# A two-layer decoder trunk on one NeuronCore: straight-line layers, weight rings in half-unit pieces, another opening and seam

## The reference, cut to what matters

```python
h = rms_norm(x, norm_g)
proj = h @ w_in                          # 1024 -> many columns
q_lat, kv_lat, z_a, dn_qkv, dn_a, dn_b, z_b, dil_qkv, z_c, gate_logits = split(proj)
y_a = mla_branch(q_lat, kv_lat, ...)     # latent attention, 4 heads; two more small projections (q_b, kv_b)
y_b = gated_deltanet_branch(dn_qkv, dn_a, dn_b, ...)   # convolution, chunked delta rule
y_c = dilated_branch(dil_qkv, ...)       # three groups of windowed attention
ys = stack([y_a * silu(z_a), y_b * silu(z_b), y_c * silu(z_c)])
branch_out = einsum('bsnc,ncd->bsnd', ys, w_branch)
mixed = sum(sigmoid(gate_logits) * branch_out)
x = x + mixed @ w_out
```

## Time and profile before

| | us |
|---|---|
| three timed runs | 909.52, 910.36, 913.64 |
| median | 910.36 |
| span of the profiled execution | 909.1 |
| TensorE busy | 863.2 (95%) |
| VectorE busy | 601.9 (66%) |
| ScalarE busy | 499.4 (55%) |
| GpSimd busy | 266.5 (29%) |
| chain that ended last: TensorE / issue / GpSimd / VectorE | 70% / 14% / 6% / 5% |

### The profile page before, as it was taken

How to read it: one execution, slowest core, us unless ns; L and a number is a source line. 1 busy time by engine, 2 the same in 40 slices (tenths; PEclk the granted TensorE clock), 3 DMA queues, 4 the chain that set the end, 5 groups by cost and what they waited for, 6 DMA issues and landing times.

```text
span 909.1 us, 13835 instructions
## 1 busy us (share of the span) xinstructions
PE 863.2 (95%) x4578; PEld 730.4 (80%) x4578; DVE 601.9 (66%) x766; ACT 499.4 (55%) x1034; POOL 266.5 (29%) x240
## 2 busy tenths in 40 slices
PE   4988999899999999999989799998899999999997
PEld 4977788778888887788778677887788888877886
DVE  5477669786566466486645874798675745765773
ACT  5776456437566554345357764655573855443542
POOL 1234012693516001241112520237543330114120
PEclk9999999999999999999989999999999999999999
DMA  8544334442524344345274243444334242443551
GB/s 252 161 135 175 106 127 139 139 135 69 167 94 133 101 138 152 127 156 215 64 215 155 93 160 119 139 140 133 105 134 134 84 154 93 139 152 127 185 185 47
DMA packets 67821, 124.51 MB, mean 137 GB/s; under 512 B 5165, under 2 KB 12327, under 8 KB 67623
## 3 DMA queue, kind: packets, MB, share of 16 engines
q1 hardware_dynamic: 67191, 122.30, 41.5%
q10 hardware_dynamic: 560, 1.30, 0.4%
HBM read 122.55 MB, written 1.05 MB: 136 GB/s over the span
## 4 chain that ended last, share of the span: by engine, by line
PE 70%; issue 14%; POOL 6%; DVE 5%; ACT 2%; DMA 1%; SPq 0%; POOLq 0%; DVEq 0%; ACTq 0%
PE bank L624 17%; PE bank L626 17%; PE bank L625 17%; POOL sm L1523 3%; PE bank L756 2%; PE bank L818 2%; PE bank L826 2%; PE bank L728 2%; PE bank L710 2%; DVE w_lo L1148 2%; PE bank L825 1%; PE bank L737 1%; PE bank L726 1%; PE bank L725 1%; PE bank L654 1%
## 5 line engine op out<-in xcount | busy, mean ns | idle before, releaser
L1148 DVE TENSOR_TENSOR w_lo<-raw,w_hi 128x1024 fp32r<-128x1024 f32 (+4 forms) x240 | 315.4, 1356 | 111.9 <-ACT w_hi L903 108.9
L624 PE MATMUL bank<-w_hi,hT 128*128 128x512 f32 (+2 forms) x800 | 318.3, 398 | 17.2 <-DVE w_lo L1148 7.2
L626 PE MATMUL bank<-w_hi,hT 128*128 128x512 f32 (+2 forms) x800 | 310.6, 388 | 0.0
L625 PE MATMUL bank<-w_lo,hT 128*128 128x512 f32 (+2 forms) x800 | 310.3, 388 | 0.0
L903 ACT ACTIVATE w_hi<-raw 128x1024 fp32r<-128x1024 f32 (+4 forms) x240 | 230.7, 1015 | 79.5 <-PE bank L626 78.1
L624 PEld LDWEIGHTS bank<-w_hi,hT 128*128 128x128 f32 x800 | 152.4, 191 | 50.2 <-DVE w_lo L1148 14.6
L626 PEld LDWEIGHTS bank<-w_hi,hT 128*128 128x128 f32 x800 | 152.0, 190 | 29.7
L625 PEld LDWEIGHTS bank<-w_lo,hT 128*128 128x128 f32 x800 | 152.4, 190 | 26.2
L1523 POOL TENSOR_TENSOR sm<-sm,tab 128x8 f32<-128x8 f32 (+2 forms) x72 | 64.5, 897 | 267.6 <-ACT at L982 110.3
L1107 ACT ACTIVATE at<-at,sm 128x128 f32<-128x128 f32 (+1 forms) x64 | 32.8, 514 | 69.1 <-DVE sm L1374 50.0
L624 PE MATMUL bank<-w_hi,yT 128*128 128x512 f32 (+1 forms) x136 | 54.8, 403 | 2.0 <-DVE w_lo L1148 2.0
(11 more groups left out here) (201 smaller groups left out, 1101.3 us busy)
## 6 DMA issues: line engine op xcount, KB each, us to landing
raw<-in_w_in SPq DMA_DIRECT2D x84, 1024.0 KB, 5.0
raw<-in_w_branch SPq DMA_DIRECT2D x12, 1024.0 KB, 5.1
raw<-in_w_out SPq DMA_DIRECT2D x8, 1024.0 KB, 5.0
raw<-in_w_in SPq DMA_DIRECT2D x4, 768.0 KB, 6.8
raw<-in_w_in SPq DMA_DIRECT2D x4, 640.0 KB, 8.2
raw<-in_mla_w_q_b SPq DMA_DIRECT2D x4, 576.0 KB, 3.9
raw<-in_mla_w_kv_b SPq DMA_DIRECT2D x4, 512.0 KB, 3.8
tab<-in_tables ACTq DMA_DIRECT2D x1, 1152.0 KB, 7.8
```

What stands on the lines that cost most here:

```text
L624: mm(o, src[0][:, k0 + k, tok], hi[:, k, :], start=starts and k == 0, stop=False)
L625: mm(o, src[0][:, k0 + k, tok], lo[:, k, :], start=False, stop=False)
L626: last = mm(o, src[1][:, k0 + k, tok], hi[:, k, :], start=False, stop=ends and k == nk - 1)
L1148: tt(view(w_lo, u % SPLIT, nk, n)[:, a:b, :], view(raw, u % RAW, nk, n)[:, a:b, :], view(w_hi, u % SPLIT, nk, n)[:, a:b, :].bitcast(F32), ...
```

## The change

It does the following.

- Both layers are written out: `ORDER` is a list of (layer, step), the loops are gone and all semaphore values are constants.
- The unit of both rings is a piece, half a unit (2 of 4 chunks; 2 and 1 of 3 for qb; 1 and 1 of 2 for kvb). The raw ring has 4 pieces (before 6), the split ring 5 (before 4). A `unit` step is now one piece; after piece q comes the `prep` of piece q + 4, which waits until TensorE is done with piece q - 1. Within a piece all chunks of t = 0 run first, then those of t = 1; so a block's bank 0 is complete half a piece before the block's end.
- latkv comes before latq. dn_g0, dn_g1, lat_norm move to unit 3 and dn_gc to unit 4.
- The opening: SP issues x first; the parameter loads go to ScalarE's queue, as does the second table load right behind; the rows' copy and the factor 0.5 are made by ScalarE; sine and exponential table come after the first four pieces' splits; VectorE's angle steps are merged; five small warm-up matmuls.
- The seam: xT 0 and 1 of the next layer come after the first unit of out1; xT 2, 3, norm and m_tables come between the two pieces of the next layer's unit 0. Layer 1's gain loads stand on SP behind the pieces of units 0 and 1 and wait for out1's adds.
- mT 2 and 3 come between the pieces of unit 56. GpSimd adds mixed per token tile. The output is stored in four parts.

```diff
-RAW, SPLIT = 3, 2
+RAW, SPLIT = 4, 5
+WARM = (3, 2)
-    us = halves("latq", 0, Q_RANK + 2 * H) + halves("latkv", 0, KV_RANK + ROPE) + halves("dn", 0, W)
+    us = halves("latkv", 0, KV_RANK + ROPE) + halves("latq", 0, Q_RANK + 2 * H) + halves("dn", 0, W)
-    put(1, ("dn_g0",), ("dn_g1",))
-    put(2, ("dn_gc",))
-    put(3, ("lat_norm",))
+    put(3, ("dn_g0",), ("dn_g1",), ("lat_norm",))
+    put(4, ("dn_gc",))
+def build_order():
+    steps, middle = step_table(), middle_table()      # middle_table: {56: [("mT", 2), ("mT", 3)]}
+    order = [(0, ("xT", 0)), (0, ("xT", 1)), (0, ("prep", 0, 0)), (0, ("prep", 0, 1)), (0, ("xT", 2)), (0, ("xT", 3)),
+             (0, ("prep", 1, 0)), (0, ("prep", 1, 1)), (0, ("norm",)), (0, ("m_tables",))]
+    def ahead(layer, u, p):
+        q = piece_at(layer, u, p) + SPLIT - 1
+        return [(q // (PIECES * NU), ("prep", q // PIECES % NU, q % PIECES))] if q < PIECES_ALL else []
+    for layer in range(DEPTH):
+        for u in range(NU):
+            order.append((layer, ("unit", u, 0)))
+            order += ahead(layer, u, 0)
+            if u == 0 and layer > 0:
+                order += [(layer, ("xT", 2)), (layer, ("xT", 3)), (layer, ("norm",)), (layer, ("m_tables",))]
+            order += [(layer, s) for s in middle.get(u, [])]
+            order.append((layer, ("unit", u, 1)))
+            order += ahead(layer, u, 1)
+            if whole(u) or UNITS[u][2] == 1:
+                order.append((layer, evict_step(u)))
+            order += [(layer, s) for s in steps[u]]
+            if u == NU - 2 and layer + 1 < DEPTH:
+                order += [(layer + 1, ("xT", 0)), (layer + 1, ("xT", 1))]
+    return order
...
 # SyncE
+                    for p in range(PIECES):
+                        q = piece_at(layer, u, p)
+                        if q >= RAW:
+                            sp.wait_ge(lo_done, q - RAW + 1)
+                        ...
-                    if u == RAW - 1:
-                        sp.wait_ge(*layer_start(layer))
+                    if u == 1:
+                        if layer > 0:
+                            sp.wait_ge(*out_taken(1, layer - 1))
                         for name, src in (("mq", mla_q_norm_g), ...
 # TensorE, one piece
+                pe.wait_ge(lo_done, q + 1)
                 for t in range(NT):
                     if starts:
                         pe.wait_ge(*free(step, layer, t))
...
+                    for k in range(k1 - k0):
+                        a = at_k + k0 + k
+                        mm(o, src[0][:, a, tok], hi[:, k, :], start=starts and k == 0, stop=False)
+                        mm(o, src[0][:, a, tok], lo[:, k, :], start=False, stop=False)
+                        last = mm(o, src[1][:, a, tok], hi[:, k, :], start=False, stop=last_piece and k == k1 - k0 - 1)
...
 # ScalarE, prep
+                act.wait_ge(raw_loaded[q % RAW], 16 * RAW_AT[q])
+                if q >= SPLIT:
+                    act.wait_ge(*used(q - SPLIT))
 # TensorE, transposes of x
-                if step[1] == 0:
-                    pe.wait_ge(*layer_start(layer))
-                pe.wait_ge(start[f"x_loaded{step[1] // 2}"], 16)
+                if layer > 0:
+                    pe.wait_ge(*out_taken(step[1] // 2, layer - 1))
+                else:
+                    pe.wait_ge(start[f"x_loaded{step[1] // 2}"], 16)
...
```

More of the change, by code:

```diff
@@ L195, in banks @@
     if k == "unit":
-        what, _, hf, _, _ = UNITS[a[0]]
-        return [0, 1] if hf == 0 else []
+        return [0, 1] if UNITS[a[0]][2] == 0 and a[1] == 0 else []
     if k in ("xT", "mT"):
@@ L494, in after, with used, block_taken, out_taken @@
         def after(engine, step, layer):
-            return part(engine, step), layer * COUNT[step[0]] + PLACE[step] + 1
+            return part(engine, step), PLACE[(layer, step)] + 1
         def bank_unit(u):
[L500 to L516, removed]
+            return ("unit", u - UNITS[u][2], 0)
+        def used(q):
+            layer, u, p = q // (PIECES * NU), q // PIECES % NU, q % PIECES
+            if ends(u, p):
+                return full(bank_unit(u), layer, 1)
+            return piece_done, q + 1 - layer * ENDS - sum(ends(v, PIECES - 1) for v in range(u))
+        def block_taken(u, layer, t=1):
+            return taken(bank_unit(u), layer, t)
+        def out_taken(i, layer):
+            return block_taken(unit_of("out", i), layer)
         def unit_of(what, i):
@@ L600, in unit @@
             def unit(step, layer):
-                u = step[1]
+                _, u, p = step
                 what, i, hf, nk, n = UNITS[u]
-                hi, lo = view(w_hi, u % SPLIT, nk, n), view(w_lo, u % SPLIT, nk, n)
-                starts, ends = whole(u) or hf == 0, whole(u) or hf == 1
-                src, k0 = (yT, 3 if what == "kvb" else 0) if whole(u) else (hT, hf * nk)
+                q = piece_at(layer, u, p)
+                k0, k1 = piece(nk, p)
+                hi, lo = view(w_hi, q % SPLIT, k1 - k0, n), view(w_lo, q % SPLIT, k1 - k0, n)
+                starts, last_piece = (whole(u) or hf == 0) and p == 0, ends(u, p)
+                src, at_k = (yT, 3 if what == "kvb" else 0) if whole(u) else (hT, hf * nk)
                 if what == "qb":
@@ L612, in unit @@
                 pair = "xT" if u < 2 else "mT" if what == "out" and i == 0 else None
+                if pair:
+                    pe.wait_ge(*taken((pair, (at_k + k0) // 2), layer))
+                pe.wait_ge(lo_done, q + 1)
                 for t in range(NT):
@@ L1506, in _ @@
             last.then_inc(start["rot_ready"], 1)
-            dve.wait_ge(start["rows_copied"], 1)
-            with dve.Fori(0, DEPTH) as layer:
-                for step in ORDER:
-                    if step[0] in parts:
-                        parts[step[0]](step, layer)
+            for layer, step in ORDER[ORDER.index((0, ("norm",))):]:
+                if step[0] in parts:
+                    parts[step[0]](step, layer)
         @block.gpsimd
@@ L1538, in evict @@
                 what, i, hf, nk, n = UNITS[u]
-                pool.wait_ge(*block_taken(u, layer))
-                m = mixed[:, :, (i % 2) * n:(i % 2 + 1) * n]
-                tt(m, m, gate, ALU.add).then_inc(part("gpsimd", step), 1)
+                for t in range(NT):
+                    pool.wait_ge(*taken(bank_unit(u), layer, t))
+                    m = mixed[:, t, (i % 2) * n:(i % 2 + 1) * n]
+                    last = tt(m, m, gate[:, t, :], ALU.add)
+                last.then_inc(part("gpsimd", step), 1)
             def norm(step, layer):
```

295 lines of the change are left out of this document (141 added, 154 removed).

## The result

The changed kernel takes 921.91 us (median of 4 runs, 921.2 to 924.89) where the kernel before takes 910.84 (4 runs beside it, 909.52 to 913.64): a ratio of 1.012, 95% interval 1.009 to 1.0151. It is slower by about 11 us, outside the 0.5% that a measurement tells. The profiled execution's span is 919.0 us (before 909.1), so 9.9 us are to be found in the trace. (A timed execution of the changed kernel lies 2.2 us above its own span, one of the kernel before 1.8 us; the rest of the 11 is scatter.)

The account below looks back on a forecast made before the run. TensorE, busy 863.2 of 909.1 us, was taken to bound the kernel, leaving some 46 us of idle time and slow matmuls to win. Terms summed to +9.3 on the median of 910.4, given as 919.5; range 902 to 927.

Parts of the forecast that it names:

- Opening: Start until dn0: loads, then ScalarE's splits and norm let q_lat begin at about 24.0 us; +0.9 us.
- qb and kvb: qb and kvb blocks, both layers: ScalarE's split ahead, waiting for its slot, delays the evictions; +4.8 us.
- The ring's gain: DeltaNet stretch, both layers: the deeper ring removes a w_lo wait, GpSimd then limits; -1.2 us.
- Late evictions: Five blocks a layer at branch and output: VectorE's split work delays evictions, 0.57 us each; +5.7 us.
- mT: First output half, both layers: moving the transposes of mixed inside it removes a 1.18 us wait; -2.4 us.
- Seam: Between layers: gain loads delay layer 1's fifth piece, whose split holds ScalarE ahead of xT 2 and 3; +1.9 us.
- "not held" bound: Between layers: the lower bound if ScalarE were not held by the fifth piece's split; -6.6 us.
- Straight-line code: Whole kernel: writing out the loop in itself changes nothing, bounds 0 and +5 us.
- the first (loads and splits ahead as meant): Faster rival: layer 1's fifth piece lands before xT 2, the seam gains 6.6 us; 897 us, chance 0.18.
- The second, losses hidden: Rival: qb-stage and VectorE eviction losses are hidden, nothing to measure; 912 us, chance 0.20.
- Slow starts: Rival: each stop of the qb and kvb stage adds 2.6 us of slow matmuls, four places; 930 us, chance 0.07.
- Loads bounding the ring: Rival: 240 piece loads of 512 KB, one behind the other, set the time; about 926 us, chance 0.05.

Follow-up runs that it names:

- run 7: The changed kernel with the positions' load second on ScalarE's queue, ahead of the parameter loads; 921.91 us, ratio 1.0121.
- Run 8: The changed kernel with four instead of five pieces in the split ring, each split one piece later in the order; 922.28 us, ratio 1.0134.
- run 10: The changed kernel with the split three pieces ahead instead of four, the split ring still of five; 916.2 us, ratio 1.0051.
- run 5: The changed kernel with the eviction ahead of the second piece's split only from unit 47 on (branch5 to out1); 917.9 us, ratio 1.0097.
- run 12: The changed kernel with splits three pieces ahead, layer 1's gain loads behind unit 3, and the tails' evictions ahead of the second split; 909.44 us, ratio 0.9993.
- Run 1: The changed kernel with layer 1's seven gain loads behind the pieces of unit 3 instead of unit 1; 914.95 us, ratio 1.0025.
- Run 4: The kernel before with its five loops over the layers written out and nothing else; 905.71 us, ratio 0.9937.
- run 11: The changed kernel with the split three pieces ahead and layer 1's gain loads behind unit 3; 909.43 us, ratio 0.9975.
- run 6: The changed kernel with the eviction ahead of the second piece's split for the two qb units alone; 928.86 us, ratio 1.0217.

## Why the prediction was right

The forecast of 919.5 was 2.4 below the measured 921.9, and inside its range; the ratio's interval (+8 to +14 us) holds it. (The terms add up to +9.3, and 910.4 + 9.3 is 919.7, not 919.5.) The mechanisms of the three largest losses, at the seam, in the qb stage and at the late evictions, are in the trace as described; that the sum comes so close is partly luck, since errors cancel. So term by term:

- **Opening, +0.9 against +0.6.** The amount held, the working did not. I had it bound by loads until 14.0; but the loads of the first stretch were in, and what was late was VectorE, whose chain of angles could begin only at 8.89, when the positions had landed as the sixth load of ScalarE's queue. It ran to 13.26 ahead of the first hT, and the norm, which I let follow at once, waited 1.91 us for VectorE's rot, so q_lat began at 26.23, not 24.0. In run 7, with the chain 2.5 us earlier, that wait is gone and q_lat starts 1.24 earlier. kv_lat, part of it at the lower clock, ended at 24.5, not near 19; so TensorE stood 1.76 us ahead of q_lat, not 5, and no slow start (2.6 in the sum) followed. Run 7 shows the other case: a stop of 3.94 and then 2.3 us of slow matmuls. Two errors of over 2 us cancelled here. (The granted clock in the earlier trace rows reads 1.00 for the opening of the kernel before, although its 392-column matmuls start every 0.33 us, the lower level; there the pitch has to be read, not that column.)
- **qb and kvb, +4.8 against +2.8.** The mechanism held, and the sum left two things out. ScalarE's timeline at the end of the first qb block, which answers to the earlier trace rows:

```profile
52.71 1.06 ACT L947 ACTIVATE w_hi<-raw 128x1024 fp32r<-128x1024 f32 x1 [1.97 <-PE bank L660]
53.68 0.35 ACT L1018 ACTIVATE at<-bank,sm 128x128 f32<-128x128 f32 x1
...
56.99 0.58 ACT L1025 ACTIVATE at<-bank,sm 128x384 f32<-128x384 f32 x1
57.47 1.05 ACT L947 ACTIVATE w_hi<-raw 128x1024 fp32r<-128x1024 f32 x1
```

  The split stands 1.97 us waiting for TensorE and then in front of the eviction; dn1 starts at 63.11, 2.9 later than before at equal work, where 1.7 was forecast. But the stop of 1.86 us that the kernel before has ahead of kvb0 (TensorE at 73.11, for VectorE) is then absorbed, which I had not looked for. And the lower clock moved: dn1's first half took 5.74 us before and 7.35 after, kvb0 4.57 before and 3.00 after. In the windows of kvb0, layer 0, before and after, the granted clock is the column ahead of the DMA share:

```profile
75.31:79.88 4.57, 4.57 (x16) 3.56 (x16) 1.40 (x3) 1.62 (x6) 2.46 (x3) 0.63 0.93 316
```

```profile
78.32:81.32 3.00, 3.00 (x16) 2.45 (x16) 1.49 (x3) 1.50 (x4) 2.57 (x1) 1.00 0.79 268
```

  I priced stops by their length and added no lower clock behind them, on either side of the comparison; here the two spells nearly cancel. Layer 1 shows the same exchange (dn1's first half 5.74 and 7.54 us, kvb0 4.49 and 3.00).
- **The ring's gain, -1.2 against -1.5.** At its own place it was smaller: at dil3 2.5 us are won in the first half and 2.3 lost in the second, in each layer, to GpSimd (L854 in the waits), so 0.2 stay of the 0.6 that were forecast. The rest of the 1.5 is a spell of lower clock at dil1 in layer 0 that went, so the nearness of -1.5 to -1.2 is chance. Run 8, with a slot less, has no w_lo wait at dil3 either, so it is not the depth that took it away. What the depth could have given went into the greater lead (run 8 against run 10).
- **Late evictions, 0.57 a block against 0.69.** Measured at z1, gate2, gate3 and out1, 0.61, 0.71, 0.72, 0.73 us. The mechanism, split ahead, its residual, then the eviction, is shown by runs 5, 10 and 12.
- **mT, -2.4: this failed.** At out0 the 1.18 us wait went, and 0.44 for VectorE's gate and 0.51 for GpSimd's mixed stand in its place, with the late bank; net 0.0. "GpSimd's add in halves is just in time" was the step that did not hold.
- **Seam, +1.9 against +3.3.** TensorE started the second unit of layer 1 at E+11.7, where E+11.6 was written. Two steps in it were off and cancelled: the fifth piece was issued at E+4.0, not E+5.9, and was there at E+9.0, 5.0 later, not 3.3. What is left is the slow start: a matmul every 0.267 us where it is 0.146 at the full clock, for 21 of them, 2.5 us where 2.2 were put in; and 0.9 for xT 0 and 1, which came into the end of out1 and which I had not counted there. Run 1's seam is 8.8 shorter; the forecast and its "not held" bound lay 8.5 apart.
- **Straight-line code, 0: this failed, and it hides in the sum.** Run 4 finds 5.8 us by the ratio and 6.1 in the trace, of which 3.2 are the seam's. I had counted 1.36 for the loop's turn and nothing for the clock. The changed kernel is straight-line code too, and measured against run 4 it is 16 us slower, not 11, and loses 6.5 at the seam, not 3.3.

Of the rivals: the first (loads and splits ahead as meant) decided where it said, at the fifth piece, and the place speaks for it: with that piece on time (runs 1 and 11) the seam is 5.6 shorter than before's, where 6.6 were put down. But even with the late evictions gone too (run 11) the kernel is at 909.4, no 897: the w_lo waits that vanish are replaced by others. The second, losses hidden, is out: each was found in the trace, if only 2.8 of the 4.8 in the qb and kvb stage. Slow starts at all four places of that stage are out as a sum: the stops there brought the lower clock mainly at dn1, 1.6 and 1.8 us a layer, and the kernel before had as much at kvb0. Loads bounding the ring is out. (The Trainium skill, "DMA: Bandwidth & Descriptors", "Rules for kernel authors", wants 1 MiB or more in a DMA; the trace agrees for one load, 3.7 us for 512 KB against 5.0 for 1024, but no load bounds the ring here.) The waits of SyncE's queue show that the loads waited for the slots, and not the slots for the loads:

```profile
SPq L611 <- DVE w_lo L1196: 768.0, 226, 11.5
```

**What stays open.** Between run 11 (909.4) and the kernel before with its loop written out (905.7) lie 4 us. Much of it is lower clock: run 4's seven executions all have a mean granted clock of 0.990 or more, run 11's only three of ten, and those three lie at 903.95 to 906.25. Of work that takes longer at the same clock, the qb and kvb stage of layer 0 has 1.5 us (from the second half of dn0 to dn2, 43.41 against 41.90 us, both at 1.00); evicting first was no cure (run 6), and running both pieces of a token tile before the next tile was not tried. It is not known what decides whether a stop brings the lower clock; it makes single profiled spans scatter, and the medians of runs 5 and 10 lie 5.3 and 4.6 above theirs, where the kernel before's lies 1.3 above.

## What to carry to other kernels

An engine with an in-order queue that waits for a slot holds back everything behind it: order the refill of a ring so that its slot has been free for a while when the engine comes to it (here one piece of lead less, in a ring of the same depth, turned 178 us of such waits into 49 and gave each tail 3 us; a slot more at the same lead gave at least 6 us, at a greater lead nothing). When a ring becomes finer, look at which small transfers now stand in front of the next piece on its queue, since the stock of loaded weights that used to cover them is smaller (here four half units in place of three whole ones). And test a change of structure by its simplest part alone: the loop written out gave 0.6%, while the rest of the change cost some 16 us.

## What was not expected of the hardware

- A loop of two turns on five engines, written out, gives 5.8 us of 911 (0.6%). In the trace that is 1.3 us of idle time at the turn, 1.9 more at the seam, where the granted clock is 1.00 (the upper level, 2.4 GHz) against 0.87, and 2.9 elsewhere, half of them spells of lower clock.
- The same 16 matmul records of kvb0 take 3.00 us at a granted clock of 1.00 and 4.57 at 0.63, the lower level (1.2 GHz) in part of them. In the kernel before this came behind idle times of 1.9 us, in both layers; with its loop written out, behind 1.8 us in both layers, only in layer 1. So a stop of 1.9 us can cost 1.5 us more in slow matmuls, and whether it does changes with edits elsewhere: a difference of 1.5 us in one stage of one trace should not be put down to an edit.
- The same order of eviction and split gave 3 us a layer at the tails and cost 47 us over the whole program: the price of an order is local.
